# Token mixing of an RWKV-7 layer: three rounded products in place of exact ones, and sums by head in column groups

## The chip, the cores and the metric

One core of one Trainium2 chip runs the whole program. The metric is the time of one execution on the device, in microseconds.

## What is computed

Two layers over 1,072 tokens (16 meta and 1,024 prompt tokens, and 8 samples of 4 tokens), width 1,024. The first layer is latent attention with a feed-forward part, the second is an RWKV-7 time mix with a feed-forward part. The change is in the second layer. Cut to what matters:

```python
x_prev = jnp.concatenate([shift_prev[:, None], h[:, :-1]], axis=1)
xx = x_prev - h
xr, xw, xk, xv, xa, xg = (h + xx * mu[j] for j in range(6))
r = xr @ w_r                                             # 1024 x 1024 each
k = xk @ w_k
v = xv @ w_v
log_w = -jax.nn.softplus(-(dw0 + jnp.tanh(xw @ dw1) @ dw2)) - 0.5   # dw1: 1024 x 64
a = jax.nn.sigmoid(aw0 + (xa @ aw1) @ aw2)               # aw1: 1024 x 64
g = jax.nn.sigmoid(xg @ gw1) @ gw2                       # gw1: 1024 x 128
kk = heads(k * k_k)
kk = kk / jnp.maximum(jnp.sqrt(jnp.sum(kk * kk, axis=-1, keepdims=True)), 1e-12)
k = heads(k * (1.0 + (a - 1.0) * k_a))
S_T, y = lax.scan(_wkv_step, wkv0, (r, decay, k, v, -kk, kk * a))
y = norm_by_head(y) + jnp.sum(r * k * r_k, axis=-1, keepdims=True) * v
out = (y * g) @ w_o
```

## The kernel before

Activations lie with the features on the 128 partitions, as eight slabs of 1,072 tokens (`nT` is the normed input, `hT` the hidden state). Tokens are cut into three pieces of 384, 384 and 304 (`PIECES`), and products go into eight PSUM banks: four in a ring that ScalarE empties (`ra`, `a_filled` and `a_drained`) and four in a ring that VectorE empties (`rv`). Each engine has its program written out by hand, and semaphores order them. A wait before an instruction holds up all that is queued behind it on that engine. At some places, at both ends of the mixing stage among them, all engines meet.

**The mixing stage** lies between two such meetings. SyncE stores `hT` to a scratch tensor and loads weights. PE sums squares for the norm, VectorE makes `nT` piece by piece (L2210, L2213). Then VectorE makes the six mixed inputs one after another, each of all tokens (`xm`, two buffers): a difference of neighbours (L2430), two repairs of first columns, and eight multiply-adds (L2437). PE takes them in the order r, w, k, a, v, g. For r, k and v it runs over four blocks of 256 weight columns (`big`, weights `wb` in two buffers), for w, a and g over one block of 128 columns (`lora_in`). All of these are products of float32 operands:

```python
for m_ in range(2):
    for at, w in PIECES:
        product(ra, lambda j: wb[par][:, j, m_ * P:(m_ + 1) * P], lambda j: x[:, j, at:at + w], KT, w=w)
```

A float32 matmul shows as two records in the trace. r and k come out with features on the partitions, v with tokens on them (weights as the moving operand, 256 columns). ScalarE copies each bank into `stage` and GpSimd stores the stage to scratch tensors, from which the next stage loads.

**The rounded product** exists in the feed-forward part (`product3`): each operand is split into a rounded float32r part (`hi`, made by ScalarE) and the rest (`lo`, made by VectorE for activations and GpSimd for weights), and three matmuls take the place of one: hi by hi, hi by lo and lo by hi. Each is one record in the trace.

**The recurrence stage** goes in chunks of 128 tokens (`chunk`), eight and a tail of 48, each in two halves of eight heads. It inverts a triangular matrix by levels (16, 32, 64), and PE does other work of the chunk (`fillers`) while ScalarE and VectorE turn one level's result into the next level's operand. Two of these fillers are sums over each head's 64 features: `bonus_sums` of this chunk and `key_sums` of the next, both by `sums_by_head`, eight matmuls that give 16 rows. `key_scales` spreads the inverse norms back over the features, and `turn_bonus` turns the bonus sums.

## Time and profile before

| | |
|---|---|
| median of 3 runs | 3864.74 us (3859.37 to 3880.96) |
| the profiled execution, its own time | 3877.49 us |
| its span | 3875.8 us |
| mean granted clock of TensorE | 0.951 of full speed |
| busy: PE, PE weight loads, VectorE, ScalarE, GpSimd | 93%, 79%, 45%, 24%, 14% of the span |
| chain that ended last, share of PE | 64% |
| memory traffic | 58 GB/s over the span |

The profile comes from one execution; positions in it are microseconds from the start of its span. In a timeline a row is a run of like instructions: start, duration, engine, line, operation, tiles written and read, count, and in brackets the idle time ahead of it with what ended it. PE is the matmul unit of TensorE and PEld its weight loads.

### The profile page before, as it was taken

To read this page: it belongs to the slowest core of one execution; us is meant where nothing else is said; L and a number is where in the kernel's file an instruction comes from. 1 tells how busy PE (TensorE), PEld (TensorE's weight loads), DVE (VectorE), ACT (ScalarE), POOL (GpSimd) and SP (SyncE) were. 2 spreads that over 40 slices of the span, in tenths; PEclk is the share of its full clock that TensorE was granted. 3 is DMA by queue.
4 is the path that set the end of the run, shared out by engine and by line. 5 is a ranking of instruction groups with operands and counts; after the bars stand their busy time and mean duration, and the time that the engine had idled before them with its cause. 6 is when DMAs were issued, how large, how long until landed. Compare 5 with 4: busy or idle time off the path is not lost.

```text
span 3875.8 us, 61931 instructions
## 1 busy us (share of the span) xinstructions
PE 3598.1 (93%) x23964; PEld 3078.7 (79%) x23964; DVE 1759.1 (45%) x3204; ACT 943.7 (24%) x1787; POOL 525.5 (14%) x220
## 2 busy tenths in 40 slices
PE   9999998998999999969999588989899899999997
PEld 6667666667999999946567477778785699999996
DVE  3545543116444444461240467655631544444444
ACT  2223324302111111111001455555520211111111
POOL 0000000001111122101000122223221121111120
PEclk9999999999999999989999789999869999999998
DMA  2222114402111111022111101000051111111101
GB/s 96 59 73 62 52 40 143 141 0 68 52 43 43 43 43 43 0 82 86 45 67 45 68 12 40 29 23 23 20 162 43 55 44 43 43 43 43 43 22 45
DMA packets 151310, 206.35 MB, mean 53 GB/s; under 512 B 42542, under 2 KB 126433, under 8 KB 150786
## 3 DMA queue, kind: packets, MB, share of 16 engines
q1 hardware_dynamic: 145122, 184.55, 14.4%
q0 software_dynamic: 6048, 19.73, 1.6%
q8 instruction: 113, 1.85, 0.2%
q14 instruction: 27, 0.22, 0.0%
HBM read 173.87 MB, written 50.82 MB: 58 GB/s over the span
## 4 chain that ended last, share of the span: by engine, by line
PE 64%; issue 7%; DVE 5%; PEld 4%; ACT 2%; DMA 1%; SPq 0%; POOL 0%; ACTq 0%; PEldq 0%; DVEq 0%; POOLq 0%
PE bank L429 61%; PEld bank L429 4%; PE bank L437 3%; DVE arena L2437 1%; DVE arena L2430 1%; ACT arena L2016 1%; DVE arena L2213 1%; DVE hT L2522 1%; DVE std L2210 0%; SPq L1260 0%; ACT arena L1943 0%; DVE n L2213 0%; DMA arena<-arena 0%; DVE arena L2456 0%; DVE arena L2504 0%
## 5 line engine op out<-in xcount | busy, mean ns | idle before, releaser
L429 PE MATMUL bank<-arena 128*128 128x384 f32 (+20 forms) x9432 | 1562.3, 351 | 142.2 <-ACT arena L1682 28.5
L429 PEld LDWEIGHTS bank<-arena 128*128 128x128 f32 (+11 forms) x9432 | 1124.7, 181 | 560.7 <-issue 171.2
L2225 DVE TENSOR_TENSOR hT<-hT,bank 128x384 f32<-128x384 f32 (+1 forms) x816 | 426.4, 526 | 523.5 <-PE bank L429 523.5
L429 PE MATMUL bank<-n_hi,up_hi 128*128 128x384 f32 (+1 forms) x1536 | 502.3, 327 | 27.2 <-DVE n_lo L2382 14.2
L1682 ACT COPY arena<-bank 128x512 f32<-128x512 f32 (+12 forms) x573 | 264.6, 497 | 1035.2 <-PE bank L429 755.4
L429 PE MATMUL bank<-u_hi,dn_hi 128*128 128x384 f32 (+1 forms) x1536 | 501.1, 326 | 0.0
L429 PE MATMUL bank<-u_lo,dn_hi 128*128 128x384 f32 (+1 forms) x1536 | 499.9, 325 | 0.0
L429 PE MATMUL bank<-n_hi,up_lo 128*128 128x384 f32 (+1 forms) x1536 | 499.6, 325 | 0.0
L429 PE MATMUL bank<-n_lo,up_hi 128*128 128x384 f32 (+1 forms) x1536 | 499.6, 325 | 0.0
L429 PE MATMUL bank<-u_hi,dn_lo 128*128 128x384 f32 (+1 forms) x1536 | 496.0, 323 | 0.0
L1521 POOL TENSOR_TENSOR up_lo<-arena,up_hi 128x2048 fp32r<-128x2048 f32 x32 | 151.2, 4725 | 1590.9 <-ACT up_hi L1838 1590.9
L2406 DVE TENSOR_TENSOR arena<-arena 128x384 f32<-128x384 f32 (+1 forms) x192 | 160.8, 837 | 437.2 <-ACT arena L1854 437.2
L429 PEld LDWEIGHTS bank<-n_hi,up_hi 128*128 128x128 f32 x1536 | 289.9, 189 | 28.1 <-issue 28.1
L429 PEld LDWEIGHTS bank<-n_lo,up_hi 128*128 128x128 f32 x1536 | 290.2, 189 | 0.0
L429 PEld LDWEIGHTS bank<-n_hi,up_lo 128*128 128x128 f32 x1536 | 289.8, 189 | 0.0
L429 PEld LDWEIGHTS bank<-u_hi,dn_lo 128*128 128x128 f32 x1536 | 289.4, 188 | 0.0
L429 PEld LDWEIGHTS bank<-u_lo,dn_hi 128*128 128x128 f32 x1536 | 288.3, 188 | 0.0
L429 PEld LDWEIGHTS bank<-u_hi,dn_hi 128*128 128x128 f32 x1536 | 288.0, 187 | 0.0
L1854 ACT ACTIVATE arena<-bank 128x384 f32<-128x384 f32 (+1 forms) x192 | 89.8, 469 | 597.6 <-PE bank L429 593.9
L437 PE MATMUL bank<-table,arena 128*128 128x128 f32 (+6 forms) x1426 | 181.5, 271 | 51.9 <-DVE arena L2213 21.9
L1521 POOL TENSOR_TENSOR dn_lo<-arena,dn_hi 128x2048 fp32r<-128x2048 f32 x32 | 147.6, 4613 | 583.2 <-ACT dn_hi L1844 583.2
L1844 ACT ACTIVATE dn_hi<-arena 128x2048 fp32r<-128x2048 f32 x32 | 61.3, 1917 | 642.6 <-PE bank L429 634.9
(181 smaller groups left out, 2903.5 us busy)
## 6 DMA issues: line engine op xcount, KB each, us to landing
arena<-in_ffn_w_up SPq DMA_DIRECT2D x32, 1024.0 KB, 5.4
arena<-in_ffn_w_down SPq DMA_DIRECT2D x32, 1024.0 KB, 7.4
arena<-past_scratch SPq DMA_DIRECT2D x32, 640.0 KB, 8.1
past_scratch<-in_cache_kv_latent SPq DMA_DIRECT2D x128, 128.0 KB, 2.4
hidden_scratch<-hT SPq DMA_DIRECT2D x1, 4288.0 KB, 13.8
past_scratch<-in_cache_k_rope SPq DMA_DIRECT2D x128, 32.0 KB, 2.1
arena<-in_rwkv_w_r SPq DMA_DIRECT2D x4, 1024.0 KB, 5.2
r_scratch<-arena POOLq DMA_DIRECT2D x8, 512.0 KB, 5.2
```

Source lines behind the costliest of these rows:

```text
L429: return pe.matmul(out, lhsT, rhs, start=first, stop=last, skip_group_check=group)
L437: return pe.transpose(out, src, ident[0:rows, 0:rows])
L1521: lo_t.add(pool.tensor_tensor(lo[:, :, :], raw[:, :, :], hi[:, :, :].bitcast(F32), ALU.subtract))
L1682: lane.do(act.copy(dst, b if view is None else view(b)), ring.drained)
L1844: lane.do(act.activation(dn_hi[:, :, :], w_dn[par][:, :, :], ACT.Copy), hi_t)
L1854: lane.do(act.activation(relu[(u_t.n - 1) % 4][:, 0:w], b[:, 0:w], ACT.Relu), ring.drained)
L2016: ins = act.copy(heads(dst, w)[rows, :, at:at + 32], heads(src, 32)[rows, :, :])
L2213: ins = dve.scalar_tensor_tensor(out=dst[:, k, at:at + w], in0=src[:, k, at:at + w], scalar=prm[:, k, row:row + 1], in1=std[:, at:at + w], ...
L2225: lane.do(dve.tensor_tensor(hT[:, k, at:at + w], hT[:, k, at:at + w], b[:, 0:w], ALU.add), ring.drained)
L2406: lane.do(dve.tensor_tensor(r, r, r, ALU.mult))
L2430: lane.do(dve.tensor_tensor(x[:, :, 1:T], nT[:, :, 0:T - 1], nT[:, :, 1:T], ALU.subtract))
L2437: ins = dve.scalar_tensor_tensor(out=x[:, k, :], in0=x[:, k, :], scalar=prm[:, k, R_MU + row:R_MU + row + 1], in1=nT[:, k, :], op0=ALU.mul ...
```

## The change

Four things change.

1. r, k and v are made by three rounded matmuls for each exact one. VectorE makes the token difference once (`DX`), then for each of r, k, v the mixed input piece by piece into `x_mix`; ScalarE rounds it into `x_hi` (which lies where `hT` was), and VectorE leaves the rest in `x_lo`, in the place of `x_mix`. ScalarE rounds each weight block into `w_hi`, GpSimd makes `w_lo`. The buffers of weights stay at two each.
2. w, a and g keep float32 products, but without mixed inputs: x times W becomes `nT` times W plus `DX` times (mu times W), two products in one accumulation, with w and a side by side in 128 columns. w and a come first, ahead of r; g comes between r and k.
3. The stage is written out block by block, where loops over two blocks stood, and pieces are the outer loop within a block.
4. In the recurrence, the sums by head are eight matmuls of 32 columns that write four groups of 32 rows of a bank, two into each. `key_scales` reads rows in two halves instead of 16 rows, and `turn_bonus` turns 128 rows instead of 16.

```diff
+            x_lo = piece("x_lo", [P, KT, T])
+            w_lo, w_hi = [[piece(f"w_{name}{i}", [P, KT, 256]) for i in range(2)] for name in ("lo", "hi")]
...
+            piece("ahead_of_x_mix", [P, 2 * KT * T + 2 * T])
+            x_mix = piece("x_mix", [P, KT, T], F32)
...
+            def lora_sums(b, weights, acts, p, first, last):
+                at, w = PIECES[p]
+                for k in range(KT):
+                    ins = mm(b[:, 0:w], weights[:, k, :], acts[:, k, at:at + w], first and k == 0, last and k == KT - 1)
+                return ins
+
...
+            three = []
+            for p in range(3):
+                pe.wait_ge(norm_s, mark["normed1"] + p + 1)
+                three.append(ra.bank(ahead=p))
+                lora_sums(three[p], w_wa, nT, p, True, False)
+            pe.wait_ge(mu_s, 1)
+            for p in range(3):
+                pe.wait_ge(dx_s, p + 1)
+                ra.done(lora_sums(three[p], w_mu, DX, p, False, True))
+            pe.drain().then_inc(lora_used, 1)
 
             mark["shift"] = ra.filled.n
             for half in range(2):
...
+            def big(m, token_major):
+                for blk in range(4):
+                    hi, lo = w_hi[blk % 2], w_lo[blk % 2]
+                    pe.wait_ge(wlo_s, 4 * m + blk + 1)
+                    for p, (at, w) in enumerate(PIECES):
+                        if blk == 0:
+                            pe.wait_ge(xlo_s, 3 * m + p + 1)
                         if token_major:
...
+                                    rows = slice(t * P, t * P + (P if t < 8 else TAIL))
...
                                     for k in range(KT):
-                                        ins = mm(b[0:w, u * 256:(u + 1) * 256], x[:, k, t * P:t * P + w], wb[par][:, k, :],
-                                                 k == 0, k == KT - 1)
+                                        mm(out, x_hi[:, k, rows], hi[:, k, :], k == 0, False)
+                                        mm(out, x_hi[:, k, rows], lo[:, k, :], False, False)
+                                        ins = mm(out, x_lo[:, k, rows], hi[:, k, :], False, k == KT - 1)
                                 ra.done(ins)
...
+                                cols = slice(m_ * P, (m_ + 1) * P)
+                                b = ra.bank()
+                                for k in range(KT):
+                                    mm(b[:, 0:w], hi[:, k, cols], x_hi[:, k, at:at + w], k == 0, False)
+                                    mm(b[:, 0:w], hi[:, k, cols], x_lo[:, k, at:at + w], False, False)
+                                    ins = mm(b[:, 0:w], lo[:, k, cols], x_hi[:, k, at:at + w], False, k == KT - 1)
+                                ra.done(ins)
+                        if blk == 3:
+                            through(xu_t)
+                    through(wbu_t)
+                    mark["blocks"].append(ra.filled.n)
 
             big(0, False)
-            lora_in(1, wl)
-            big(2, False)
...
-            big(4, True)
-            lora_in(5, wg)
+            pe.wait_ge(wl_s, 48)
+            pe.wait_ge(mu_s, 2)
+            for p in range(3):
+                b = ra.bank()
+                lora_sums(b, w_g, nT, p, True, False)
+                ra.done(lora_sums(b, w_mu, DX, p, False, True))
+            big(1, False)
+            big(2, True)
             meet(pe, here)
             pe.wait_ge(mixw_s, mixw_n)
             pe.wait_ge(zero_s, 2)
...
             def sums_by_head(bank, w):
-                at = MIXTAB["head_cols"][0] + 14
-                for k in range(8):
-                    ins = mm(bank[0:RH, 0:w], mixtab[:, at - 2 * k:at - 2 * k + RH], kx[:, k, 0:w], k == 0, k == 7)
+                for j in range(2):
+                    at = MIXTAB["head_cols"][0] + 2 - 2 * j
+                    for g in range(4):
+                        ins = mm(bank[32 * g:32 * g + 32, 0:w], mixtab[:, at:at + 32], kx[:, 4 * j + g, 0:w], j == 0, j == 1)
                 return ins
 
...
             def key_scales(c, w):
 
                 inv_b.wait(pe, c)
-                for half in range(2):
-                    b = rv.bank()
-                    for k in range(4):
-                        ct = 4 * half + k
-                        ins = mm(b[:, k * w:(k + 1) * w], mix("head_rows", RH)[:, ct * P:(ct + 1) * P], kn_sum[0:RH, 0:w], True, True)
+                pair = [rv.bank(ahead=1), rv.bank(free=True)][::-1]
+                ends = []
+                for k in range(4):
+                    for z in range(2):
+                        rows, ct = slice(z * RN, (z + 1) * RN), 4 * (k // 2) + 2 * z + k % 2
+                        ends.append(mm(pair[z][:, k * w:(k + 1) * w], mix("head_rows")[rows, ct * P:(ct + 1) * P], kn_sum[rows, 0:w], True, True))
+                for ins in ends[-2:]:
                     rv.done(ins)
 
...
             def turn_bonus(w, summed_at):
                 apart(a_drained, ra.filled.value(ra.filled.n - summed_at))
                 b = ra.bank(free=ra.filled.n - summed_at <= 3)
-                ra.done(turn(b[0:w, 0:RH], bonus_rows[0:RH, 0:w], RH))
+                ra.done(turn(b[0:w, 0:P], bonus_rows[:, 0:w], P))
 
...
+            sp.wait_ge(norm_s, mark["normed1"] + 3)
+            load(w_g, A["rwkv_g_w1"][0].rearrange("(k p) n -> p k n", p=P), wl_t)
+            for n in range(2, 12):
+                sp.wait_ge(wb_used, n - 1)
+                load_block(n)
...
+            def split_weights(n):
+                par = n % 2
+                pool.wait_ge(whi_s, n + 1)
+                pool.tensor_tensor(w_lo[par][:, :, :], w_raw[par][:, :, :], w_hi[par][:, :, :].bitcast(F32), ALU.subtract).then_inc(wlo_s, 1)
...
+            split_weights(0)
+            for n in range(12):
+                if n + 1 < 12:
+                    split_weights(n + 1)
+                store_block(n)
...
+            def round_weights(n):
+                par = n % 2
+                wb_t[par].expect(16)
+                act.wait_ge(wb_s[par], wb_t[par].n)
+                act.activation(w_hi[par][:, :, :], w_raw[par][:, :, :], ACT.Copy).then_inc(whi_s, 1)
+
+            def round_mixed(m, p):
+                at, w = PIECES[p]
+                act.wait_ge(xm_s, 3 * m + p + 1)
+                act.activation(x_hi[:, :, at:at + w], x_mix[:, :, at:at + w], ACT.Copy).then_inc(xhi_s, 1)
+
+            round_weights(0)
+            act.wait_ge(hid_s, 16)
+            round_mixed(0, 0)
+            round_mixed(0, 1)
+            for at, w in PIECES:
+                b = ring.bank()
+                act.activation(lora[0:64, at:at + w], b[0:64, 0:w], ACT.Tanh)
+                lane.do(act.copy(lora[64:P, at:at + w], b[64:P, 0:w]), ring.drained)
...
+            round_mixed(0, 2)
...
+                if n >= 2:
+                    act.wait_ge(stg_s[par], stored[par])
...
+                for p, (at, w) in enumerate(PIECES):
...
+                    if p == 0 and n + 1 < 12:
+                        if n >= 1:
+                            act.wait_ge(wb_used, n)
+                        round_weights(n + 1)
+                    if blk == 3 and m < 2 and p > 0:
+                        round_mixed(m + 1, p - 1)
+                if blk == 3 and m < 2:
+                    round_mixed(m + 1, 2)
...
+            dve.wait_ge(wl_s, 32)
+            for half, row in ((0, 1), (1, 4)):
+                cols = slice(64 * half, 64 * half + 64)
+                ins = dve.tensor_tensor(w_mu[:, :, cols], w_wa[:, :, cols], prm[:, :, R_MU + row:R_MU + row + 1].broadcast_to([P, KT, 64]), ALU.mult)
+            ins.then_inc(mu_s, 1)
...
+            for at, w in PIECES:
+                first = max(at, 1)
+                ins = dve.tensor_tensor(DX[:, :, first:at + w], nT[:, :, first - 1:at + w - 1], nT[:, :, first:at + w], ALU.subtract)
...
+                ins.then_inc(dx_s, 1)
...
+            def mixed(m, p):
+                at, w = PIECES[p]
+                row = (0, 2, 3)[m]
+                if m > 0:
+                    dve.wait_ge(xm_used, 3 * m - 3 + p + 1)
                 for k in range(KT):
-                    ins = dve.scalar_tensor_tensor(out=x[:, k, :], in0=x[:, k, :], scalar=prm[:, k, R_MU + row:R_MU + row + 1],
-                                                   in1=nT[:, k, :], op0=ALU.mult, op1=ALU.add)
-                lane.do(ins, xm_t)
+                    ins = dve.scalar_tensor_tensor(out=x_mix[:, k, at:at + w], in0=DX[:, k, at:at + w], scalar=prm[:, k, R_MU + row:R_MU + row + 1],
+                                                   in1=nT[:, k, at:at + w], op0=ALU.mult, op1=ALU.add)
+                ins.then_inc(xm_s, 1)
+
+            def split_mixed(m, p):
+                at, w = PIECES[p]
+                dve.wait_ge(xhi_s, 3 * m + p + 1)
+                dve.tensor_tensor(x_lo[:, :, at:at + w], x_mix[:, :, at:at + w], x_hi[:, :, at:at + w].bitcast(F32), ALU.subtract).then_inc(xlo_s, 1)
+
+            for m in range(3):
+                mixed(m, 0)
+                mixed(m, 1)
+                split_mixed(m, 0)
+                mixed(m, 2)
+                split_mixed(m, 1)
+                split_mixed(m, 2)
+                if m == 0:
+                    dve.wait_ge(lora_used, 1)
+                    dve.wait_ge(wl_s, 48)
+                    dve.tensor_tensor(w_mu[:, :, :], w_g[:, :, :], prm[:, :, R_MU + 5:R_MU + 6].broadcast_to([P, KT, P]), ALU.mult).then_inc(mu_s, 1)
             meet(dve, here)
             dve.wait_ge(mixw_s, mixw_n)
```

PE at the start of the mixing stage, after the second feed-forward loop. In the kernel before (`bank` numbers are those of the ring of four, 9x128 are the turned shift rows):

```order
L429 MATMUL bank3<-arena,table 128x304 [waits a_drained,squares_ready]
L429 MATMUL bank3<-arena,table 128x304 x7
L437 MATMUL bank0<-table,arena 9x128 [waits a_drained,normed_ready]
L437 MATMUL bank0<-table,arena 9x128 x3
L437 MATMUL bank1<-table,arena 9x128 [waits a_drained]
L437 MATMUL bank1<-table,arena 9x128 x3
L799 UNCONDITIONAL_BRANCH [waits mixed_ready,w_lora_loaded]
```

The same place in the changed kernel:

```order
L443 MATMUL bank0<-arena 128x384 [waits a_drained,normed_ready,w_lora_loaded]
L443 MATMUL bank0<-arena 128x384 x7
...
L443 MATMUL bank2<-arena 128x304 [waits differences]
L443 MATMUL bank2<-arena 128x304 x7
L451 MATMUL bank3<-table,arena 9x128 [waits a_drained]
L451 MATMUL bank3<-table,arena 9x128 x3
L451 MATMUL bank0<-table,arena 9x128 [waits a_drained]
L451 MATMUL bank0<-table,arena 9x128 x3
L443 MATMUL bank1<-x_hi,w_hi0 128x384 [waits a_drained,mixed_split,w_mix_split]
L443 MATMUL bank1<-x_lo,w_hi0 128x384
L443 MATMUL bank1<-x_hi,w_lo0 128x384
```

The w and a products have moved ahead of the turns, into banks 0 to 2, and the second turn and the first product of r each need one of these banks back from ScalarE.

ScalarE at that place in the changed kernel (`w_hi` and `x_hi` are the roundings, 64x384 and 64x304 are w and a leaving the banks):

```order
L1919 ACTIVATE w_hi<-arena 128x2048 [waits w_mix_loaded0]
L1924 ACTIVATE x_hi<-x_mix 128x8x384 [waits mixed_ready,hidden_stored]
L1924 ACTIVATE x_hi<-x_mix 128x8x384 [waits mixed_ready]
L1932 ACT_TABLE_LOAD
L1932 ACTIVATE arena<-bank 64x384 [waits a_filled]
L1933 COPY arena<-bank 64x384
L1932 ACTIVATE arena<-bank 64x384 [waits a_filled]
L1933 COPY arena<-bank 64x384
L1932 ACTIVATE arena<-bank 64x304 [waits a_filled]
L1933 COPY arena<-bank 64x304
L1711 COPY arena<-bank 9x512 [waits a_filled] x2
L1924 ACTIVATE x_hi<-x_mix 128x8x304 [waits mixed_ready]
```

In the kernel before, the two copies of 9x512 followed directly on the norm; now two roundings and the emptying of three banks stand ahead of them.

PE in the first half of a chunk, before:

```order
L437 MATMUL bank1<-table,arena 64x64 [waits a_drained]
L437 MATMUL bank1<-table,arena 64x64 x7
L429 MATMUL bank5<-arena 16x128 [waits v_drained,keys_squared]
L429 MATMUL bank5<-arena 16x128 x7
L429 MATMUL bank2<-table 128x256 [waits a_drained]
L429 MATMUL bank2<-arena,hT 64x64 [waits a_drained]
```

And in the changed kernel:

```order
L451 MATMUL bank2<-table,arena 64x64 [waits a_drained]
L451 MATMUL bank2<-table,arena 64x64 x7
L443 MATMUL bank5<-arena 32x128 [waits v_drained,keys_squared]
L443 MATMUL bank5<-arena 32x128 x7
L443 MATMUL bank3<-table 128x256 [waits a_drained]
L443 MATMUL bank3<-arena,hT 64x64 [waits a_drained]
```

The order is the same; the eight matmuls of `key_sums` write 32 rows each where they wrote 16.

## Rows read from the trace of the kernel before

**Rows 1.** Stages by time: us, busy us and instructions by engine, clock, DMA share.
```profile
907.70:1660.10 752.40, 752.40 (x4608) 752.15 (x4608) 374.19 (x682) 104.78 (x128) 143.19 (x31) 1.00 0.11 39
...
1660.70:2135.40 474.70, 426.55 (x1544) 290.88 (x1544) 136.03 (x93) 50.41 (x91) 29.15 (x40) 0.95 0.20 66
```

**Rows 2.** Timeline of DVE at the start of the stage: start us, us, instruction.
```profile
1687.10 3.66 DVE L2213 SCALAR_TENSOR_TENSOR arena<-hT,prm,std 128x304 f32<-128x304 f32 x8
...
1690.79 9.08 DVE L2430 TENSOR_TENSOR arena<-arena 128x8568 f32<-128x8568 f32 x1
...
1700.30 10.05 DVE L2437 SCALAR_TENSOR_TENSOR arena<-arena,prm 128x1072 f32<-128x1072 f32 x8
```

**Rows 3.** Timeline of PE, second feed-forward end to first product.
```profile
1663.55 16.30 PE L429 MATMUL bank<-arena,table 128*128 128x384 f32 x48 [3.45 <-ACT arena L1689]
...
1710.80 14.53 PE L429 MATMUL bank<-arena 128*128 128x384 f32 x40 [18.11 <-DVE arena L2437]
```

**Rows 4.** Timeline of PE through the products of k and v.
```profile
1850.64 31.04 PE L429 MATMUL bank<-arena 128*128 128x384 f32 x96 [5.08 <-DVE arena L2437]
...
1881.92 29.09 PE L429 MATMUL bank<-arena 128*128 128x384 f32 x96 [0.24 <-issue]
...
1970.81 14.65 PE L429 MATMUL bank<-arena 128*128 128x384 f32 x48 [0.63 <-ACT arena L1682]
...
1990.54 33.44 PE L429 MATMUL bank<-arena 128*128 128x256 f32 x144 [5.08 <-DVE arena L2437]
...
2120.26 14.65 PE L429 MATMUL bank<-arena 128*128 128x384 f32 x48 [0.63 <-ACT arena L1682]
```

**Rows 5.** Timeline of PE, end of the feed-forward part: single rounded matmuls.
```profile
1649.73 0.33 PE L429 MATMUL bank<-u_lo,dn_hi 128*128 128x384 f32 x1
...
1653.05 0.34 PE L429 MATMUL bank<-u_hi,dn_lo 128*128 128x384 f32 x1
...
1653.22 0.30 PE L429 MATMUL bank<-u_hi,dn_hi 128*128 128x304 f32 x1
...
1659.80 0.30 PE L429 MATMUL bank<-u_hi,dn_lo 128*128 128x304 f32 x1
```

**Rows 6.** Tiles and lines of the feed-forward split: ns min/median/max.
```profile
L1859 ACT ACTIVATE n_hi<-n x6: 2238/2753/2763, 893.9 to 3072.3; 128x3072 fp32r<-128x3072 f32 x4, 128x2432 fp32r<-128x2432 f32 x2
L2382 DVE TENSOR_TENSOR n_lo<-n,n_hi x6: 2680/3346/3353, 904.1 to 3075.5; 128x3072 fp32r<-128x3072 f32 x4, 128x2432 fp32r<-128x2432 f32 x2
...
L1844 ACT ACTIVATE dn_hi<-arena x32: 1915/1917/1917, 919.2 to 3774.3; 128x2048 fp32r<-128x2048 f32 x32
...
L1521 POOL TENSOR_TENSOR up_lo<-arena,up_hi x32: 4616/4628/7734, 898.5 to 3753.1; 128x2048 fp32r<-128x2048 f32 x32
```

**Rows 7.** DMA issues: KB each, us to landing.
```profile
v_scratch<-arena POOLq DMA_DIRECT2D x4, 1024.0 KB, 5.8
```

**Rows 8.** Timeline of PE, one chunk of the recurrence.
```profile
2432.47 5.53 PE L429 MATMUL bank<-arena 64*128 64x128 f32 x32 [3.07 <-issue]
...
2447.08 2.60 PE L429 MATMUL bank<-arena 128*16 128x128 f32 x16
...
2451.01 1.15 PE L429 MATMUL bank<-arena 64*64 64x64 f32 x32 [0.69 <-ACT arena L2035]
...
2453.60 1.92 PE L429 MATMUL bank<-arena 128*16 128x128 f32 x16
...
2456.08 1.14 PE L429 MATMUL bank<-arena,hT 64*64 64x64 f32 x16
...
2458.15 1.90 PE L429 MATMUL bank<-std,hT 128*128 128x64 f32 x16
```

**Rows 9.** Timeline of ACT, the same chunk.
```profile
2454.49 0.56 ACT L1682 COPY arena<-bank 64x512 f32<-64x512 f32 x1
...
2457.86 1.28 ACT L1963 ACT_TABLE_LOAD   x1
```

**Rows 10.** Timeline of PE, cached attention: sums in column groups.
```profile
646.84 1.00 PE L429 MATMUL bank<-arena 128*32 128x128 f32 x24
```

More of the change, by code:

```diff
@@ L778, in _ @@
                 ra.done(ins)
-            mark["mixing"] = ra.filled.n
-            wb_t, xm_t, xu_t, wbu_t = [Tally(s) for s in wb_s], Tally(xm_s), Tally(xm_used), Tally(wb_used)
-            pe.wait_ge(wl_s, 48)
-            def mixed(n):
-                xm_t.expect()
-                pe.wait_ge(xm_s, xm_t.n)
-                return xm[n % 2]
-            def through(tally):
-                tally.add(pe.drain())
-            def lora_in(n, weights):
-                x = mixed(n)
-                for at, w in PIECES:
-                    product(ra, lambda j: weights[:, j, :], lambda j: x[:, j, at:at + w], KT, w=w)
-                through(xu_t)
@@ new lines, in _ @@
+            stored = [0, 0]
+            for n in range(12):
+                m, blk, par = n // 4, n % 4, n % 2
+                if n == 1:
+                    act.wait_ge(out_s, out_n + 32)
+                if n >= 2:
+                    act.wait_ge(stg_s[par], stored[par])
+                stored[par] += 32 if m == 2 else 64
+                for p, (at, w) in enumerate(PIECES):
+                    if m == 2:
+                        for tiles in [(3 * p, 3 * p + 1), (3 * p + 2,)] if p < 2 else [(6, 7), (8,)]:
+                            rows = P if tiles[0] < 8 else TAIL
+                            take(stage[par][0:rows, tiles[0] * 256:(tiles[-1] + 1) * 256], rows, 256 * len(tiles))
+                    else:
+                        for m_ in range(2):
+                            take(stage[par][:, m_ * T + at:m_ * T + at + w], P, w)
+                    if p == 0 and n + 1 < 12:
[6 more added lines that the diff above has]
+                    round_mixed(m + 1, 2)
+                if n == 3:
+                    for at, w in PIECES:
+                        b = ring.bank()
+                        lane.do(act.activation(gate[:, at:at + w], b[:, 0:w], ACT.Sigmoid), ring.drained)
```

202 lines of the change are left out of this document (75 added, 127 removed).

## Prediction

> **What bounds the kernel now.** I read the table of stages first. In the feed-forward part PE is busy for all of 752.40 us at full clock; the mixing stage takes 474.70 us with PE busy for 426.55 of them [rows 1]. So PE sets the pace of this stage too, and what is not PE's work are gaps. Next the timelines. The stage opens with a chain on VectorE: norm to 1690.76, the first mixed input (9.08 us of differences, 10.05 us of multiply-adds) to 1710.35 [rows 2], and PE's first product starts at 1710.80, after 18.11 us of idling [rows 3]. Then PE is dense up to 2134.91, except that it waits 5.08 us for VectorE twice, and each time the product behind the gap takes 1.95 us longer than its like (31.04 against 29.09 us), since it begins at half clock [rows 4]. Behind the stage the recurrence first waits for its own loads, which the change doesn't touch.
>
> **A matmul's price, before.** A block of r or k is 48 float32 matmuls, 96 records, 29.09 us: 0.606 us each. A block of v is 72 matmuls of 256 columns. Four of them with their gaps run from 1990.54 to 2120.26, 129.72 us. A product of 128 columns by all tokens (w, a, g) is 14.65 us [rows 4].
>
> **A rounded matmul's price.** The feed-forward part is made of them: 4,608 in 752.40 us [rows 1], 0.1633 us each on the mix of pieces that r and k have too (two of 384 to one of 304). One by one: 19 steps of 384 columns from 1649.73 to 1653.05 are 0.1747 us each, 47 steps of 304 from 1653.22 to 1659.80 are 0.1400 us [rows 5]. Three for one thus cost 0.490 against 0.606 us. A block of r or k: 144 x 0.1633 = **23.5 us**.
>
> v moves 256 columns, which no row shows rounded. By the line through the two widths (0.434 ns a column) it is 0.119 us. From below, 16 records that move only 64 columns behind full weight loads take 1.90 us, 0.119 us each with the last one's tail [rows 8]: the weight loads alone set about this pace. From above, it can't be more than the 0.140 us of 304 columns. I take 0.120, 216 x 0.120 = **25.9 us** a block, and keep up to 30.2. On this the Trainium skill (TensorE: Matmul & The Clock Gate, LDWEIGHTS) says that a load takes its columns over 1.2 GHz, 107 ns for 128, whatever the rows. That is as long as 256 columns move at 2.4 GHz, so by the page v would run at about 0.109 us and end 9 us earlier; the rows above have no record behind a full load at that pace, and I stay with them.
>
> **The stage after, step by step.**
> - *w and a first.* PE's norm sums end at 1679.85 [rows 3]. Three `nT` products follow, each when its piece is normed; the last starts at 1690.8 and ends at 1694.9. VectorE goes on at 1690.76 with the two weight scalings (1,024 elements at the 1.06 ns of the difference, 1.2 us) and the differences, 9.1 + 0.5 us in three pieces. PE takes them at 1695.5 and ends at 1709.9 (14.4 us). The work that was idle time before costs nothing here.
> - *Start of r.* VectorE is free at 1702.1. A mixed piece of 384 costs 4.3 us (between the 3.66 of 304 and the 10.05 of 1,072 columns [rows 2]), so pieces stand at 1706.4 and 1710.7. ScalarE rounds them in 2.75 us each, VectorE's rest takes 3.35 [rows 6]: `x_lo` of piece 0 at 1714.1. But ScalarE empties the banks of w and a only behind its second rounding (1713.5), with a table load of 1.28 us and then about 1 us a piece (two passes; one of 512 columns takes 0.56) [rows 9]. The second turn and r's first bank wait for that: r starts at **1716.9**, 2.8 us later than `x_lo` alone asks. PE has then idled some 5 us, so I add 2.0 us for half clock, as [rows 4] show behind 5.08 us.
> - *r, k:* 4 x 23.5 each, and 0.4 us at each of the eight seams (0.24 and 0.63 in [rows 4]): 191.2, with the 2.0: 193.2 us.
> - *g* between them: two products in place of one, 29.3 us. Under it all of k's splitting is hidden: after r's last block VectorE needs about 10 us more.
> - *From k to v* nothing lies between. VectorE gets piece 1 to work on when PE is through with it, 6.7 us ahead of k's end; multiply-add 4.3 and rest 3.35 us end 1 us behind k's end. A wait of 1.2 us, and none for pieces 1 and 2, since v's piece 0 lasts 8.6 us.
> - *v:* 4 x 25.9 + 1.2 of seams = 104.8.
> - Sum: 1716.9 + 193.2 + 29.3 + 1.2 + 104.8 = 2045.4.
> - *End.* The last store was hidden under g; now it stands bare: copy 0.4, issue 1.5, landing 5.8 us [rows 7]. The stage ends at **2053**, not 2135.4: **-82 us**.
>
> What covers the rest: in a block of 23.5 us ScalarE rounds the next weights (1.9 us) behind piece 0's banks, at 9 us, and GpSimd splits them in 4.6, at worst 7.7 us [rows 6]: done by 19 us. If that cover goes, each of eleven seams grows. The weight load, issued at the block's start, has 9 us to land; a store of that size takes 5.8 [rows 7]. Going from exact to rounded leaves ring waits as they are: a bank fills in 3.4 to 4.2 us and is emptied in 0.6.
>
> **The recurrence.** Column groups have their like in the cached attention: 24 records of 32-column weights in 1.00 us [rows 10], 0.042 us each, against 1.92 us for 16 records of `key_sums` now [rows 8]. New: 0.7 us. `key_sums` would end 1.2 us sooner, but the next step needs ScalarE's copy, which ends at 2455.05 [rows 9] and PE got to it at 2456.08 [rows 8]: 0.9 us are worth having. `bonus_sums` (2.60 us) saves nothing, because PE already waits 0.69 us for ScalarE behind it [rows 8]; that wait grows. `turn_bonus` (two records of 128 columns, +0.15 us) eats into the same slack. `key_scales` pairs halves of 64 rows; such records take 5.53 us for 32 [rows 8], partly at half clock, so I put it at nothing, from -0.5 to +0.5 a chunk. Operations on 128 partitions in place of 16 have the same length along the free axis. Eight chunks: **-8 us**, with the first chunk's slow start; bounds -16 and +6. The Trainium skill (TensorEngine Tiling, Key Properties) warns that a change of tiling mode drains the array. That would add two drains to each sum; the 24 records above stand between full-size turns and still took 1.00 us, so it is in my price.
>
> **Sum.** -82 - 8 = -90 us. Against the profiled execution's own 3877.5 us that is 3787; it stands 12.8 us over the median of the runs shown, and the median moves to about **3775 us**.
>
> **Rivals.**
> - *Weight loads pace v* (0.140 us) and the seams grow to 1.5 us: +17 +12: 3804. For: the bare-load pace of [rows 8] is as high as my price. Against: none seen at 304 columns. 0.13.
> - *The recurrence gains all of it*, because ScalarE, itself fed by PE, moves forward too: another -15 us, 3760 and below. Against: the wait for ScalarE in [rows 8]. 0.09.
> - *The unrolled code is not supplied in time.* The stage's loops become some 2,000 rounded matmuls written out, and PE waits 3.07 us for issue where the recurrence's loop turns back [rows 8]. Were each block to lose 3 us so, the gain falls to 54 us (3811); the sign turns at 7.5 us a block, 0.22 us a rounded matmul, and at 10 us a block it is 3895. Against: attention's short records, also written out, come at 0.042 us [rows 10]. 0.03 for slower.
> - *It does not do what it says:* rounded matmuls with x as the stationary operand, or behind two alternating buffers, take as long as exact ones (0.202 us each), and the time is that of before, less the idle start and more g and the store: within 0.5%. 0.03.
> - The forecast, 3750 to 3800: 0.72.
>
> **Range.** 3745 to 3812 takes in the forecast and most of the first two rivals. A measurement of this kernel can tell about 0.5% (19 us) from no change. Faster by more than that: 0.94; within: 0.03; slower: 0.03.
>
> **What would show it right or wrong.** In the changed trace: first r matmul near 1717, blocks of 23.5 and 25.9 us, one 29.3 us product between r and k, no wait over 2 us at the start of v, the meeting at 2053, `key_sums` at 0.7 us and a longer wait for ScalarE behind `bonus_sums`. I am wrong if rounded matmuls of 256 columns are slower than 0.14 us, if the seams show waits for GpSimd's `w_lo` or VectorE's `x_lo`, or if the clock drops in the recurrence because PE now has less to fill it with.

## The result, and the profile after

The changed kernel takes 3814.0 us (median of 4 runs, 3802.6 to 3817.5) against 3870.4 us before (4 runs): ratio 0.985, 95% interval 0.9812 to 0.9887. It is faster, by 56 us, where 90 were forecast, and lies 2 us above the forecast range. The profiled execution took 3812.1 us, against 3877.5.

The stage table of the changed kernel, columns as in [rows 1] (stretch, us, then busy us and instructions of PE, weight loads, VectorE, ScalarE and GpSimd, the granted clock, DMA share and GB/s):

```profile
907.70:1660.10 752.40, 751.94 (x4608) 751.69 (x4607) 374.44 (x683) 104.87 (x128) 143.18 (x31) 1.00 0.12 39
1660.70:2057.00 396.30, 374.13 (x2264) 340.00 (x2264) 108.24 (x116) 94.58 (x112) 85.00 (x52) 0.98 0.24 80
```

The mixing stage answers to the second of [rows 1]. Its inside is seen in the timeline of PE (start, duration, instruction, in brackets the idle time ahead and what ended it); the rows are the opening of the stage, the first matmul of blocks of r, g's products (six rows like the one shown, to 1847.78), and the first matmuls of v's blocks:

```profile
1679.18 5.32 PE L443 MATMUL bank<-arena 128*128 128x384 f32 x16
1688.93 26.25 PE L443 MATMUL bank<-arena 128*128 128x384 f32 x80 [4.43 <-DVE arena L2247]
1715.28 0.61 PE L451 MATMUL bank<-table,arena 128*9 128x128 f32 x4
1719.08 0.61 PE L451 MATMUL bank<-table,arena 128*9 128x128 f32 x4 [3.19 <-ACT arena L1933]
1720.17 0.42 PE L443 MATMUL bank<-x_hi,w_hi 128*128 128x384 f32 x1 [0.47 <-ACT arena L1933]
...
1745.74 0.42 PE L443 MATMUL bank<-x_hi,w_hi 128*128 128x384 f32 x1 [0.26 <-issue]
...
1818.71 5.40 PE L443 MATMUL bank<-arena,std 128*128 128x384 f32 x16 [0.37 <-issue]
...
1944.87 0.36 PE L443 MATMUL bank<-w_hi,x_hi 128*128 128x256 f32 x1 [0.71 <-DVE x_lo L2493]
...
1970.91 0.36 PE L443 MATMUL bank<-w_hi,x_hi 128*128 128x256 f32 x1 [0.26 <-issue]
...
2069.34 6.47 PE L443 MATMUL bank<-arena 64*128 64x128 f32 x32 [19.86 <-DMA arena<-in_rwkv_ln_b]
```

From block to block of v is 26.04 us, of which 0.26 is the seam; the last matmul of v ends at 2049.49. From the first sum of the norm to the first matmul of the recurrence it was 483.97 us (1663.55 in [rows 3] to 2147.52); it is 406.25 (1663.09 to 2069.34): 77.7 us less. The mixing stage did nearly what was forecast.

The recurrence did not. I measure it from its first matmul to VectorE's sixteenth new state (line 2743, one in each half of a chunk): 673.4 us before, **687.7 us** now, 14.3 us more. A half is the stretch from one new state to the next; the first half of each chunk holds the sums by head. One of them shows why. The timeline of PE in the first half of the fourth chunk:

```profile
2365.22 2.05 PE L443 MATMUL bank<-arena 64*128 64x128 f32 x16
2368.39 1.15 PE L443 MATMUL bank<-arena,hT 64*64 64x64 f32 x32 [1.12 <-ACT arena L2050]
2369.47 0.65 PE L443 MATMUL bank<-arena 128*32 128x128 f32 x16
2372.09 0.70 PE L443 MATMUL bank<-table 128*128 128x256 f32 x2 [1.98 <-ACT arena L1976]
2374.14 1.97 PE L443 MATMUL bank<-arena 64*64 64x64 f32 x32 [1.34 <-ACT arena L2069]
...
2378.29 1.08 PE L443 MATMUL bank<-arena 128*32 128x128 f32 x16
2379.30 1.22 PE L443 MATMUL bank<-table 128*128 128x256 f32 x2
...
2390.57 7.95 PE L443 MATMUL bank<-arena 128*128 128x64 f32 x34
```

The third row is `bonus_sums` in column groups: 0.65 us where 16 records took 2.60 in [rows 8] and 1.92 in other chunks. Behind it PE waits 1.98 us for ScalarE, runs the dummy matmul of `keep_busy` (whose result nobody reads; the kernel before has it too), and waits 1.34 us again. The next 32 small matmuls take 1.97 us where [rows 8] has 1.15, and all rows down to 2400 are as slow as that, the last one shown at 0.234 us a record; `key_sums` (the sixth row) takes 1.08 us, not 0.65. TensorE has gone to half clock, 1.2 GHz, behind a stretch of 4.7 us in which it worked 1.35, and stays there for 26 us. The stretches of four halves in the stage table:

```profile
2314.36:2352.26 37.90, 33.77 (x377) 29.35 (x378) 31.80 (x61) 20.76 (x42) 9.21 (x6) 0.91 0.12 43
2352.26:2400.97 48.71, 42.10 (x381) 36.94 (x380) 19.22 (x27) 25.27 (x58) 12.86 (x6) 0.72 0.04 12
2400.97:2438.88 37.91, 34.44 (x382) 30.04 (x383) 31.34 (x62) 18.86 (x37) 8.43 (x5) 0.91 0.13 46
2438.88:2475.16 36.28, 31.27 (x375) 26.89 (x375) 18.65 (x27) 23.28 (x53) 10.99 (x6) 0.95 0.04 13
```

The second of them is the half above: 48.7 us at clock 0.72. The other halves behind the first chunk and up to there take 36.3 to 37.9. Of the later halves two more are like it (49.7 us at 0.67, 47.2 at 0.68), and in the first chunk the same happens at 2131.

The long fall is not the only one. In the other first halves PE does the same work between the same waits, and the clock falls there too, but is back within 4 us. The timeline of PE one chunk earlier (36.7 us at clock 0.95):

```profile
2292.86 0.65 PE L443 MATMUL bank<-arena 128*32 128x128 f32 x16
2295.57 0.70 PE L443 MATMUL bank<-table 128*128 128x256 f32 x2 [2.07 <-ACT arena L1976]
2297.61 1.86 PE L443 MATMUL bank<-arena 64*64 64x64 f32 x32 [1.34 <-ACT arena L2069]
...
2301.46 0.64 PE L443 MATMUL bank<-arena 128*32 128x128 f32 x16
```

And in the half of 49.7 us the clock is low already in the row ahead of the sums (1.97 us), back for the dummy, and low for long only from 2537:

```profile
2530.10 1.97 PE L443 MATMUL bank<-arena,hT 64*64 64x64 f32 x32 [1.03 <-ACT arena L2050]
2532.01 1.08 PE L443 MATMUL bank<-arena 128*32 128x128 f32 x16
2533.89 0.70 PE L443 MATMUL bank<-table 128*128 128x256 f32 x2 [0.81 <-ACT arena L1976]
2535.93 1.35 PE L443 MATMUL bank<-arena 64*64 64x64 f32 x32 [1.34 <-ACT arena L2069]
```

The kernel before has short falls as well, at the same place with its old sums, and none there that lasts:

```profile
2365.08 1.92 PE L429 MATMUL bank<-arena 128*16 128x128 f32 x16
2367.79 0.70 PE L429 MATMUL bank<-table 128*128 128x256 f32 x2 [0.79 <-ACT arena L1943]
2369.83 1.85 PE L429 MATMUL bank<-arena 64*64 64x64 f32 x32 [1.34 <-ACT arena L2035]
```

So what is new is that four of the falls last. What decides whether one lasts 4 or 26 us, no run here shows.

Grouped by line over the recurrence, the wait ahead of the dummy matmuls has gone from 4.7 to 12.8 us, 1.0 us more in each chunk:

```profile
L443 PE MATMUL bank<-table 128*128 128x256 f32 x144 | 56.6, 480 | 12.8 <-ACT arena L1976 12.8
```

### The profile page after: what moved, and what is told of

The parts are those of the page before. It is cut to its first block, busy times and chain, and to the rows that moved or that the text cites. A ratio compares the mean times of both kernels' runs of the same rounds, so it can differ in the third digit from the quotient of the medians.

```text
span 3810.2 us, 63203 instructions
## 1 busy us (share of the span) xinstructions
PE 3550.0 (93%) x24684; PEld 3131.7 (82%) x24684; DVE 1730.9 (45%) x3227; ACT 989.5 (26%) x1808; POOL 581.3 (15%) x232
## 4 chain that ended last, share of the span: by engine, by line
PE 64%; issue 5%; PEld 5%; DVE 5%; ACT 2%; DMA 1%; SPq 0%; POOL 0%; ACTq 0%; PEldq 0%; DVEq 0%; POOLq 0%
PE bank L443 61%; PEld bank L443 5%; PE bank L451 3%; DVE arena L2247 1%; ACT arena L2050 1%; DVE hT L2588 1%; DVE std L2244 1%; SPq L1290 0%; ACT arena L1976 0%; DVE x_mix L2486 0%; DVE n L2247 0%; DMA arena<-arena 0%; DVE arena L2522 0%; DVE arena L2570 0%; ACT L1976 0%
## 5 line engine op out<-in xcount | busy, mean ns | idle before, releaser
L443 PE MATMUL bank<-arena 64*128 64x128 f32 (+18 forms) x8088 | 1191.4, 344 | 119.5 <-ACT arena L1711 24.5
L443 PEld LDWEIGHTS bank<-arena 128*128 128x128 f32 (+7 forms) x8088 | 865.8, 184 | 424.0 <-issue 139.8
L451 PE MATMUL bank<-table,arena 128*128 128x128 f32 (+5 forms) x1426 | 184.7, 274 | 44.0 <-DVE arena L2247 11.0
```

The lines of the kernel that those rows point to most:

```text
L443: return pe.matmul(out, lhsT, rhs, start=first, stop=last, skip_group_check=group)
L451: return pe.transpose(out, src, ident[0:rows, 0:rows])
```

## The experiments

"Recurrence" is always the stretch just defined. Positions ahead of the mixing stage differ by up to 12.5 us between executions, so stages are compared by their own lengths; these come from the one profiled execution of each kernel. "A fall" is from here on one of the long ones. Theory: the short `bonus_sums` leave PE idle for ScalarE, and the clock falls and stays low. Rivals: the new mixing stage shifts the recurrence against its loads; or the new operations of ScalarE and VectorE around the sums are longer.

**mixing_only**: the changed kernel with the sums by head of before (the cut shows the sums; their table, `key_scales`, `turn_bonus` and what reads them go back with them).

```diff
-                for j in range(2):
-                    at = MIXTAB["head_cols"][0] + 2 - 2 * j
-                    for g in range(4):
-                        ins = mm(bank[32 * g:32 * g + 32, 0:w], mixtab[:, at:at + 32], kx[:, 4 * j + g, 0:w], j == 0, j == 1)
+                at = MIXTAB["head_cols"][0] + 14
+                for k in range(8):
+                    ins = mm(bank[0:RH, 0:w], mixtab[:, at - 2 * k:at - 2 * k + RH], kx[:, k, 0:w], k == 0, k == 7)
```

> The changed kernel with the recurrence's sums by head as before (16 rows, no column groups); the mixing stage as changed. Clock theory (the shorter bonus sums leave PE idle while it waits for ScalarE, and its clock then falls to half for about 20 us at a time): the recurrence is back at the length of before, 673 us from its first matmul to the last half-state of chunk 7 where the changed kernel has 688, and the time falls to about 3798. Rival (the new mixing stage hands the recurrence a colder or worse start): the recurrence stays at 688 and the time at 3814.

3803.3 us, ratio 0.9808 (0.9777 to 0.9839); recurrence 662.4 us. The mixing stage alone is worth 72 us of the median. Its median is 11 us under that of the whole change, with intervals that overlap; its recurrence is 25.3 us shorter. No fall behind the sums is left. But I expected the 673 us of the kernel before, and it is 11.0 less with the same recurrence code (granted clock 0.90 against 0.88, and PE waits 1.61 and 2.07 us for issue where the loop turns back, against 3.07 and 3.22). So the new stage ahead does change how the recurrence runs, with the old sums for the better.

**heads_only**: the kernel before with the diff above the other way round.

> The kernel before with only the sums by head in column groups. Clock theory: the recurrence takes about 688 us in place of 673, some chunks 74 and others 87 us, and the kernel is slower than before by about 14 us (3884). Rival (the loss comes from the mixing stage): the recurrence gains my forecast 8 us or more and the time is 3862 or less.

3877.1 us, ratio 0.9992 (0.9973 to 1.0012); recurrence 674.9, with two halves of 48.8 and 47.2 us at clock 0.67 and 0.68. I expected 688 and 3884: the falls come with the sums behind either mixing stage, but two of them here and four behind the new stage. The sums cost 1.5 us of recurrence here (673.4 to 674.9) and 25.3 there (662.4 to 687.7). The first rival is out as the cause of the falls; how many there are does depend on the stage ahead, and how, no run shows.

**bonus_thrice**: the changed kernel, with the eight matmuls issued three times into the same bank (each pass starts the bank anew).

```diff
-                ra.done(sums_by_head(ra.bank(), w))
+                b = ra.bank()
+                for _ in range(3):
+                    ins = sums_by_head(b, w)
+                ra.done(ins)
```

> The changed kernel with the eight matmuls of the bonus sums done three times over into the same bank (the result is that of the last time); 24 records more of 0.04 us in each of nine places. Clock theory: PE is occupied about as long as before ahead of the wait for ScalarE, no chunk falls to half clock there, all chunks take about 74 us, and the time is about 3814 - 36 = 3778. Rival (the slow chunks come from the wait itself or from another engine, not from how busy PE is): nothing gained, 3814.

3773.3 us, ratio 0.9725 (0.9688 to 0.9762), recurrence 643.4: forty us gained by doing more. The timeline of PE at the same place as above, and the same half in the table:

```profile
2367.32 1.15 PE L443 MATMUL bank<-arena,hT 64*64 64x64 f32 x32 [1.03 <-ACT arena L2053]
2368.40 1.52 PE L443 MATMUL bank<-arena 128*32 128x128 f32 x48
2371.11 0.70 PE L443 MATMUL bank<-table 128*128 128x256 f32 x2 [1.20 <-ACT arena L1979]
2373.15 1.15 PE L443 MATMUL bank<-arena 64*64 64x64 f32 x32 [1.34 <-ACT arena L2072]
```

```profile
2351.07:2389.02 37.95, 31.47 (x413) 27.37 (x413) 19.27 (x27) 23.27 (x53) 11.60 (x6) 1.00 0.06 16
```

PE resumes at the same distance from the first row (5.83 us here, 5.75 there), so the repeats cost nothing, and in this half the clock stays. The half is 10.8 us shorter; the four halves that had a fall give 10.8 + 10.8 + 12.0 + 10.5 = 44.0 of the 44.4 us between 687.74 and 643.36 (from unrounded lengths). In most of the first halves the clock still falls for 3 to 4 us. The second rival is out too: ScalarE and VectorE have the same work as in the changed kernel (361.3 and 418.6 us busy, against 361.6 and 417.6).

**bonus_twice**: as above with `range(2)`.

> The changed kernel with the bonus sums issued twice in place of three times, about 1.1 us of PE work in place of 0.64 (once) and 1.5 (three times). If the falls come whenever the stretch around the bonus sums is less busy than some amount, they vanish all at once between the two; I expect twice to be enough for most of them, one fall left at most: about 3785 us, recurrence about 655 us. If each missing tenth of a microsecond costs its share, the time lies halfway: about 3794 us, 665 us. If twice is too little: 3814 us and three falls.

3794.4 us, ratio 0.9794 (0.9751 to 0.9836), recurrence 666.9. The time lies halfway, as the second reading had it, but not for its reason: of the four falls two are gone whole and two are left whole (48.8 us at 0.72, 50.1 at 0.67). That is one execution: the four that were timed go from 3773.5 us at a mean granted clock of 0.954 to 3804.6 at 0.944, so the number of falls probably changes from one to the next. In late_split below, whose recurrence code is that of the changed kernel, the same four halves fall again (687.3 us).

**dummy_fill**: `bonus_sums` once; three dummy matmuls behind them in the first half.

```diff
-                keep_busy(ra)
+                keep_busy(ra, 3 if d == 0 else 1)
```

> The changed kernel with its bonus sums issued once, as they are, but three dummy matmuls in place of one at the wait behind them (first half's level of 32 only, 1.1 us more of PE work). If any work of PE in that place keeps the clock, the falls vanish as in bonus_thrice: recurrence about 645 us, 3776 us. Rival, it must be the bonus sums or the time ahead of the first wait: three falls stay, 687 us, 3815 us.

3771.1 us, ratio 0.9739 (0.969 to 0.9789), recurrence 642.3. It need not be the sums: dummy matmuls behind the first of the two waits do as well.

**key_thrice**: `key_sums` three times, `bonus_sums` once.

> The changed kernel with the key sums issued three times and the bonus sums once: the same PE work added as in bonus_thrice, about 4 us later in the half, where ScalarE's copies are waited for less. If the place matters, the falls stay, and each chunk gets at most 0.9 us longer: 687 to 695 us of recurrence, 3814 to 3822 us. Rival, it is only how much PE does in the half: falls gone, 3780 us.

3800.4 us, ratio 0.9802 (0.9748 to 0.9855), recurrence 669.3: between the two expectations. Two first halves take 44.9 and 46.1 us at 0.81. The timeline of PE in the first of them:

```profile
2376.60 1.50 PE L443 MATMUL bank<-arena 64*64 64x64 f32 x32 [1.34 <-ACT arena L2072]
...
2380.28 2.79 PE L443 MATMUL bank<-arena 128*32 128x128 f32 x48
...
2385.19 1.16 PE L443 MATMUL bank<-arena 128*128 128x128 f32 x8
```

The clock still falls ahead of the key sums, but is back right behind them, at 2384, some 7 us after it fell and not 26. Work at this place shortens a fall and does not prevent it.

**heads_thrice**: heads_only with the bonus sums three times.

> The kernel before with the sums by head in column groups, and the bonus sums' eight matmuls issued three times into the same bank; the mixing stage is the old one. If the short bonus sums are what lets TensorE's clock fall in the recurrence, whatever the stage before it, then the recurrence up to its sixteenth new state takes about 643 us as in bonus_thrice (674.9 in heads_only), and the whole about 3877 - 31 = 3846 us. Rival, the repeated sums help only behind the new mixing stage: no change to heads_only, 3877 us.

3856.6 us, ratio 0.9949 (0.9928 to 0.9969), recurrence 650.5. The halves of 48.8 and 47.2 us are gone, but two of 42.5 and 41.9 at 0.88 came. The remedy works behind the old stage as well, 10 us less well than expected. Those two halves begin where the recurrence's loop turns back, and PE waits there for issue for 2.10 + 2.36 and 1.59 + 2.40 us, where it waits 1.82 and 1.60 in bonus_thrice: some 2.5 of the 4.6 and 4.3 us that they are longer. The rows around these waits run in part at half clock. Why the issue waits differ, no run shows.

**old_heads_dummy**: mixing_only with the edit of dummy_fill, to size the new sums where the clock falls for neither form.

> The new mixing stage with the old sums by head (as mixing_only), and three dummy matmuls in place of one behind the bonus sums (as dummy_fill): this is the new and the old form of the sums compared where neither lets the clock fall. dummy_fill took 642.2 us from the start of the recurrence to its sixteenth new state and 3771.1 us in all. If the new form is worth what the blind forecast gave it (8 us), this kernel takes 650 us and 3779. If it is worth what undisturbed halves show (38.0 against 36.7 and 38.7 against 37.9, 2.1 us a chunk), it takes 658 us and 3788. Rival: the longer old sums are in nobody's way, 643 and 3772.

3795.1 us, ratio 0.9795 (0.9767 to 0.9823), recurrence 662.0. Here the stretches of the recurrence of the changed kernel, of dummy_fill and of mixing_only, in this order:

```profile
2069.34:2757.08 687.74, 585.35 (x6068) 509.81 (x6069) 417.58 (x740) 361.62 (x779) 161.40 (x81) 0.82 0.08 26
```

```profile
2074.40:2716.65 642.25, 544.75 (x6100) 472.56 (x6101) 417.58 (x740) 361.15 (x779) 161.62 (x81) 0.89 0.09 28
```

```profile
2081.07:2743.50 662.43, 568.32 (x6068) 494.20 (x6069) 416.56 (x740) 361.12 (x779) 161.50 (x81) 0.90 0.09 27
```

In sum dummies do nothing for the old sums (662.4 and 662.0), which fill the place by their length; within it, a half of 42.8 us at 0.84 in mixing_only became one of 38.3, and the last half went from 37.4 to 41.5 at 0.79. Old against new form is 662.0 against 642.3, 20 us, of which this last half holds some 6 that may be chance. So in this kernel the column groups save 14 to 20 us of work and wait, and the falls that they bring cost 44, which fits the 25.3 us between mixing_only and the changed kernel.

**fuller**: bonus_thrice and dummies at the other waits of a chunk.

```diff
             def before_keys(c, ar):
+                if c > 0:
+                    keep_busy(ra, 2)
                 b_b.wait(pe, c)
...
-                    keep_busy(rv)
+                    keep_busy(rv, 3)
...
-                keep_busy(ra)
+                keep_busy(ra, 3 if d == 0 else 1)
```

> bonus_thrice with more dummy matmuls at the waits that are left: three in place of one where the second half's first level waits 1.70 us for VectorE, two new ones ahead of the 1.45 us wait for the next chunk's keys, three in place of one in the first half's level of 32. If the clock of 0.91 to 0.95 in the undisturbed halves comes from these gaps, the second halves gain some 2.5 us each and the first ones 1 us: eight chunks, about -25 us, 3750 us, clocks near 1.0. Rival, the waits only partly wait and the dummies push back what is behind them: 0.5 us for each of the 4 added places in a chunk, +10 us, 3785 us.

3759.8 us, ratio 0.9709 (0.9684 to 0.9733), recurrence 631.5. Nine of the fifteen halves behind the first now show a clock of 1.00, as the theory has it. Two neighbouring rows of the stage table:

```profile
2311.58:2348.08 36.50, 33.49 (x388) 28.69 (x388) 31.74 (x61) 20.76 (x42) 9.53 (x6) 1.00 0.13 46
2348.08:2386.68 38.60, 33.57 (x414) 29.37 (x413) 19.06 (x27) 23.27 (x53) 11.24 (x6) 0.96 0.05 15
```

But second halves, like the first of these rows, gain 1.4 us (37.9 to 36.5) where I expected 2.5: 12 us in all, half of the forecast. VectorE is busy there for 31.7 of 36.5 us, so it may be the next to set the pace; no run tests that.

**late_split**: the changed kernel with GpSimd's first `w_lo` held until the norm is through.

```diff
+            pool.wait_ge(norm_s, mark["normed1"] + 3)
             split_weights(0)
```

> The changed kernel with GpSimd's first split of a weight block held back until the three norm pieces are made. Port theory (VectorE's 128x384 multiply-adds took 8.60 in place of 4.32 us because GpSimd's 4.50 us subtraction ran at that time): the piece is back at 4.32 us, and the first product of r starts 3 to 4 us earlier; the time falls by 3 us, less than the spread between runs. Rival (VectorE waits for something else there): the piece stays at 8.60.

This is about the 4.43 us in PE's opening rows. There VectorE needed 8.60 us for a norm piece that took 4.32 before, while GpSimd worked beside it. Timelines of VectorE and GpSimd in the changed kernel:

```profile
1673.45 4.32 DVE L2247 SCALAR_TENSOR_TENSOR arena<-hT,prm,std 128x384 f32<-128x384 f32 x8
...
1680.28 8.60 DVE L2247 SCALAR_TENSOR_TENSOR arena<-hT,prm,std 128x384 f32<-128x384 f32 x8
```

```profile
1681.84 4.50 POOL L1565 TENSOR_TENSOR w_lo<-arena,w_hi 128x2048 fp32r<-128x2048 f32 x1 [62.37 <-ACT w_hi L1919]
```

late_split took 3821.4 us, ratio 0.9859 (0.9811 to 0.9907). The norm piece is back at 4.33 us, but a small operation of VectorE that takes 0.17 us elsewhere now takes 4.48 us. The first matmul of r comes 56.99 us behind the norm's first sum, as in the changed kernel (57.08), and not 3 to 4 us earlier as expected: the stall went along with the subtraction. GpSimd's subtraction starts at 1693.65, while VectorE is at work on two-input operations that take no longer than in the changed kernel; it takes 8.69 us: GpSimd was held up first, and VectorE's small operation then waited for it. The Trainium skill (SBUF — State Buffer, SBUF: two separate sides) says of the port pair that VectorE and GpSimd share: whichever starts first, an operation of VectorE with two inputs in SBUF (or in a two-port mode) or one of GpSimd, has the pair for its whole instruction, and the other waits. The trace agrees for the norm piece, which has two such inputs. The operation of 0.17 us has one, and whether it runs in a two-port mode no run here shows.

**start_early**: bonus_thrice, with VectorE making the first `w_lo` and ScalarE emptying the banks of w and a first.

```diff
-            round_mixed(0, 1)
             for at, w in PIECES:
                 b = ring.bank()
                 act.activation(lora[0:64, at:at + w], b[0:64, 0:w], ACT.Tanh)
                 lane.do(act.copy(lora[64:P, at:at + w], b[64:P, 0:w]), ring.drained)
+            round_mixed(0, 1)
...
-            split_weights(0)
...
                 mixed(m, 0)
+                if m == 0:
+                    dve.wait_ge(whi_s, 1)
+                    dve.tensor_tensor(w_lo[0][:, :, :], w_raw[0][:, :, :], w_hi[0][:, :, :].bitcast(F32), ALU.subtract).then_inc(wlo_s, 1)
```

> bonus_thrice with two edits at the start of the mixing stage: VectorE and not GpSimd makes the first w_lo (2.3 us on VectorE, behind the first mixed piece), and ScalarE empties the banks of w and a ahead of rounding the second mixed piece. If GpSimd's subtraction is what doubled VectorE's multiply-adds of the norm (8.60 for 4.32 us), that piece is back at 4.3 us; VectorE comes out 2.0 us ahead, and PE no longer waits for ScalarE's banks (3 us): r starts about 52 us after the first norm sum (57.1 in the changed kernel), and the time falls by 5 us to 3768. Rival, the chain through x_lo is as late as the banks: r starts 2 us sooner at most, 3771.

3773.5 us, ratio 0.9751 (0.9728 to 0.9774). In the timelines of VectorE and of PE:

```profile
1687.96 4.32 DVE L2249 SCALAR_TENSOR_TENSOR arena<-hT,prm,std 128x384 f32<-128x384 f32 x8
...
1713.04 2.29 DVE L2501 TENSOR_TENSOR w_lo<-arena,w_hi 128x2048 fp32r<-128x2048 f32 x1
```

```profile
1722.93 0.66 PE L443 MATMUL bank<-x_hi,w_hi 128*128 128x384 f32 x1 [4.00 <-DVE x_lo L2495]
```

The stall is gone, and r starts 52.04 us behind the norm's first sum, as expected. The stage gains 3.8 us (402.6 against 406.4 in bonus_thrice) and not 5.1, since r now runs at half clock for its first 5.5 us, behind 4.00 us of idling; in the changed kernel it does so for 3.2 us. The median shows none of it (3773.3 in bonus_thrice): 0.1% is below what it can tell.

**fuller_start**: both together.

> fuller and start_early together. The start gave 5.0 us (first norm sum to first r 52.04 against 57.08 us) of which the half clock at r's start takes back some, the filled waits gave 12 us in the recurrence; they lie in different stages and should add up: recurrence 631.5, r's start 52 us behind the norm's first sum, 3756 us, 0.970 of before. Rival, a different start shifts where the clock falls: one or two falls of 12 us come back, 3768 to 3780.

3760.1 us, ratio 0.9713 (0.9665 to 0.9761); stage 402.6 us, recurrence 632.9. The same as fuller within the interval. These two beat the changed kernel by 54 us and mixing_only by 43.

## Why the prediction was right or wrong

- *Stage, -82 us:* measured -77.7. A block of r or k: forecast 23.5, measured 23.77 between the seams, the fourth of each 24.52. A block of v: 25.9 against 25.78 (the fourth 26.52). g 29.3 against 29.07. k to v 1.2 against 0.71. Seams 0.4 against 0.26. The wait for loads ahead of the recurrence grew by 7.25 us (12.61 to 19.86), where the bare store was put at 7.7. *Start of r* is the term that was off: 1720.2 against 1716.9, since I took VectorE's norm pieces from before and gave GpSimd's split to the time beside them for nothing. [Rows 6] had the sign of it, a split of 7.7 us where the median is 4.6. What followed was right: `x_lo` was not last, ScalarE's banks were (3.19 and 0.47 us).
- *Recurrence, -8 us:* measured +14.3. This is the step that failed, as it stands there: "`bonus_sums` (2.60 us) saves nothing, because PE already waits 0.69 us for ScalarE behind it [rows 8]; that wait grows." The wait grew as said, by 1.0 us a chunk, and saved nothing. But I priced a longer wait at zero. With it the clock stayed at 1.2 GHz for some 26 us in four halves, 10.5 to 12.0 us lost in each, 44 us in all. [Rows 8] also misled me on the size of the wait: in that chunk the sums ran partly at half clock and filled it; in the ordinary chunk shown above PE waits 0.79 and 1.34 us behind sums of 1.92. The falls of the kernel before in [rows 4] and of the slow first chunk were before me; I named the fall in the last paragraph as a way to be wrong and gave it neither a price nor a chance. The Trainium skill (TensorE: Matmul & The Clock Gate, A second HAM failure mode) says that frequent short pauses between groups of matmuls are enough to make the clock go back and forth. The runs here agree: no pause in the timeline of the fourth chunk is over 2 us, and the clock goes both ways in every chunk.
- *The sums themselves* were sized too low: 14 to 20 us where the clock holds, not 8. `key_sums` took 0.65 us as forecast (0.7), but undisturbed first halves are 1.3 us shorter (38.0 to 36.7) and second ones 0.8 (38.7 to 37.9), where I allowed 0.9 and nothing. The rival that the recurrence gains all of it (-23) was nearer on this term. In the sum the two errors work against each other: 44 us of falls, less what the sums saved beyond my 8 and the 11 us that the new stage took off the recurrence, leave the 22 below.
- *The rivals of the stage:* v runs at 25.78 / 216 = 0.119 us a matmul, my price, and not at the 0.140 of the rival; no block waits for code (0.26 us of issue at a seam), and a rounded matmul costs what I took it to cost. The estimate of 0.109 us from the Trainium skill (TensorE: Matmul & The Clock Gate, LDWEIGHTS) was too fast; the measurement decides.
- *Sum:* against the forecast's -90 us the profiled executions show -65.6 of span (3810.2 from 3875.8): 4.3 us from the stage, 22.3 from the recurrence; the parts ahead and behind moved by 0.5 and 1.7 us the other way.

## What to carry to other kernels

A filler that makes PE look busy while it waits may be doing its work by being long. Before shortening one, read the granted clock of the stretch and how much PE still does there, and do not price the wait that takes its place at zero: put in what the work behind it would take at half clock, with a chance; a few dummy matmuls in the gap gave back 43 us here. And ask of each two-input operation given to GpSimd what VectorE does at that moment.

## What was not expected of the hardware

- How unlike two falls behind the same work can be: PE work of 0.65 and 0.70 us in a stretch of 4.7 us was followed by 26 us at half clock at 2374, and by less than 4 us at 2297. With 0.44 us more of work in the stretch (32 records in 1.08 us) two of the four long falls were gone in the execution profiled, with 0.88 us more (48 in 1.52 us) all four; short ones were left.
- The half clock can last under full load: from 2374 to 2400 PE is at work for nearly all of the time, at half clock. In key_thrice, with 2.8 us of 32-column matmuls on end, full clock was back after some 7 us (from 2377 to 2384).
- GpSimd's subtraction of 2,048 elements stopped VectorE for its whole length: 8.60 us for 4.32, or 4.48 us for an operation of 0.17 us. On VectorE itself it takes 2.29 us.
